# Choosing 16 experts of 16384, tile by tile and from 80 candidate pairs, in a two-block model kernel

## What is computed

```python
q = (xb @ w_q).reshape(PEER_BLOCK, PEER_HEADS, 2, PEER_HALF)
s = jnp.einsum('thjd,hjkd->thjk', q, sub_keys).astype(jnp.float32)
sv, si = lax.top_k(s, PEER_TOPK)
cand = sv[:, :, 0, :, None] + sv[:, :, 1, None, :]
cs, ci = lax.top_k(cand.reshape(PEER_BLOCK, PEER_HEADS, PEER_TOPK * PEER_TOPK), PEER_TOPK)
i1 = jnp.take_along_axis(si[:, :, 0], ci // PEER_TOPK, axis=-1)
i2 = jnp.take_along_axis(si[:, :, 1], ci % PEER_TOPK, axis=-1)
eidx = i1 * PEER_N_KEYS + i2
g = jax.nn.softmax(cs, axis=-1)
act = jax.nn.gelu(jnp.einsum('td,thkd->thk', xb, expert_u[eidx]), approximate=False)
return jnp.einsum('thk,thkd->td', (g * act), expert_v[eidx])
```

## Time and profile before

| | us |
|---|---|
| three runs | 2925.65, 2932.58, 2934.63 |
| median | 2932.58 |
| profiled execution: its time | 2928.44 |
| profiled execution: span from first to last instruction | 2926.6 |
| busy: PE, DVE, POOL, ACT | 2019.9, 1854.2, 1261.4, 638.5 |
| chain that ended last | PE 41%, DVE 23%, DMA 13%, issue 10%, POOL 7%, ACT 5% |
| moved by DMA | 797.62 MB, of it 536.94 by gathers |

### The profile page before, as it was taken

How to read it: one execution, slowest core, us unless ns; L and a number is a source line. 1 busy time by engine, 2 the same in 40 slices (tenths; PEclk the granted TensorE clock), 3 DMA queues, 4 the chain that set the end, 5 groups by cost and what they waited for, 6 DMA issues and landing times.

```text
span 2926.6 us, 26514 instructions
## 1 busy us (share of the span) xinstructions
PE 2019.9 (69%) x9256; PEld 1629.7 (56%) x9256; DVE 1854.2 (63%) x3630; ACT 638.5 (22%) x1713; POOL 1261.4 (43%) x1060
## 2 busy tenths in 40 slices
PE   7999989860887787796550031246348899993898
PEld 6888878750776676785440021234346555443685
DVE  2333310198688899867799978888976566754200
ACT  4555520110443433200210020011012200002210
POOL 0000000006576666566655656767755675641000
PEclk8999989985899888897875566665777999996899
DMA  4332324334799999899897579999987899984176
GB/s 165 110 128 108 115 94 146 109 141 171 259 353 368 347 361 370 330 414 382 316 378 266 183 278 411 358 362 335 387 321 282 322 381 390 406 322 172 63 253 245
DMA packets 178871, 797.62 MB, mean 273 GB/s; under 512 B 20001, under 2 KB 20257, under 8 KB 153137
## 3 DMA queue, kind: packets, MB, share of 16 engines
q0 software_dynamic: 147456, 536.94, 48.7%
q1 hardware_dynamic: 30704, 256.89, 23.1%
q10 hardware_dynamic: 576, 2.10, 0.2%
HBM read 793.75 MB, written 2.10 MB: 272 GB/s over the span
## 4 chain that ended last, share of the span: by engine, by line
PE 41%; DVE 23%; DMA 13%; issue 10%; POOL 7%; ACT 5%; DVEq 0%; ACTq 0%
PE ps L678 41%; DMA ring<-in_pu,eidx 9%; POOL ring L650 7%; DMA ring<-in_pv,eidx 3%; DVE acc L1833 3%; DVE junke L1833 3%; DVE junke L1827 2%; DVE acc L1827 1%; DVE si L1415 1%; DVE tmpx L1485 1%; DVE ci L1415 1%; DVE sv L1413 1%; DVE cv L1413 1%; ACT L1032 1%; ACT L1030 1%
## 5 line engine op out<-in xcount | busy, mean ns | idle before, releaser
L650 POOL DMA_INDIRECT ring<-in_pu,eidx x512 | 654.4, 1278 | 366.0 <-DVE dots L1827 221.3
L650 POOL DMA_INDIRECT ring<-in_pv,eidx x512 | 575.2, 1124 | 367.7 <-DVE acc L1833 121.5
L678 PE MATMUL ps<-uT,wr 128*128 128x256 f32 (+1 forms) x2304 | 533.6, 388 | 2.8 <-ACT ynT L1212 2.8
L678 PEld LDWEIGHTS ps<-uT,wr 128*128 128x128 f32 x2304 | 440.4, 193 | 72.1 <-issue 3.3
L678 PE MATMUL ps<-hT,wr 128*128 128x128 f32 (+2 forms) x1984 | 406.0, 369 | 8.7 <-ACT hT L1071 7.1
L678 PE MATMUL ps<-junk,h 128*128 128x128 f32 x256 | 49.5, 380 | 484.6 <-DVE junk L1436 484.6
L678 PEld LDWEIGHTS ps<-hT,wr 128*128 128x128 f32 x1984 | 304.1, 198 | 109.9 <-issue 8.1
L1827 DVE CUSTOM_DVE_ANT_0 junke<-ring,u 128x1024 f32<-128x1024 f32 x256 | 312.7, 1222 | 62.8 <-DMA ring<-in_pu,eidx 60.1
L1827 DVE CUSTOM_DVE_ANT_0 acc<-ring,u 128x1024 f32<-128x1024 f32 x256 | 313.0, 1222 | 43.2 <-DMA ring<-in_pu,eidx 40.3
L1833 DVE SCALAR_TENSOR_TENSOR acc<-ring,wgt,acc 128x1024 f32<-128x1024 f32 x252 | 324.9, 1289 | 12.1 <-DMA ring<-in_pv,eidx 12.0
L1833 DVE SCALAR_TENSOR_TENSOR junke<-ring,wgt,junke 128x1024 f32<-128x1024 f32 x252 | 325.0, 1290 | 8.3 <-DMA ring<-in_pv,eidx 8.2
(11 more groups left out here) (260 smaller groups left out, 2502.5 us busy)
## 6 DMA issues: line engine op xcount, KB each, us to landing
wr<-in_wg SPq DMA_DIRECT2D x32, 1536.0 KB, 9.0
wr<-in_wgu SPq DMA_DIRECT2D x44, 1024.0 KB, 6.2
wr<-in_wsc SPq DMA_DIRECT2D x16, 1536.0 KB, 8.5
wr<-in_wso SPq DMA_DIRECT2D x16, 1536.0 KB, 8.2
wr<-in_wq SPq DMA_DIRECT2D x16, 1152.0 KB, 5.4
wr<-in_wqku SPq DMA_DIRECT2D x18, 1024.0 KB, 8.2
wr<-in_wdn SPq DMA_DIRECT2D x12, 1536.0 KB, 7.9
wr<-in_wgate SPq DMA_DIRECT2D x16, 1024.0 KB, 5.0
```

What stands on the lines that cost most here:

```text
L650: e.indirect_dma_start(ring[k % NR][:], None, A[which], bass.IndirectOffsetOnAxis(ap=eidx[:, t, j:j + 1], axis=0)).then_inc(gathered[k % N ...
L678: return e.matmul(o, l, r, start=start, stop=stop, skip_group_check=True)
```

## The change

- A `top` unit now belongs to one tile and one head: `top16` on three pieces, that head's two halves (128 values) and the *preceding* head's pairs (80 values). The unit of head 0 has no pairs; a new unit `toplast` does those of head 7 alone. The unit `pairs` is gone.
- The 256 sums become 80 in three pieces: the best of the first half with all 16 of the second (16), the next 7 with the first 8 (56), the last 8 with the best (8). `ci` then is a place among the 80, and `slots` decodes it into the two places with ten small operations; `first` loses its two.
- Only the first tile of a pass is searched while PE makes scores. The second tile's eight `top` units and its `toplast` follow after the first tile's `index`, with the experts that the planner finds between them.

The planner's counts of experts ahead of a unit:

| unit | before | now |
|---|---|---|
| `index` of tile 1 | 13 | 45 |
| start of mixer pass 1 | 16 | 48 |
| end of its scan | 244 | 273 |
| start of choice 1 | 358 | 390 |
| first `top` of choice 1 | 367 | 399 |
| `index` of tile 2 / of tile 3 | 479 / 493 | 472 / 513 |
| start of attention of tiles 0, 1 | 512 | 516 |
| start of attention of tile 2 / of feed-forward 0 to 2 | 769 / 825 | 773 / 829 |
| last unit of that feed-forward | 1005 | 1009 |

The core of the diff:

```diff
         if hj % 2:
-            pl.add("top", q, hj // 2, v=2 * nt * 5 * (0.1 + 128 / 960.0))
-            yield True
-            pl.add("pairs", q, hj // 2, v=nt * (vc(32) + vc(256) + 5 * (0.1 + 256 / 960.0)))
+            pl.add("top", q, hj // 2, t0, v=10 * (0.1 + 128 / 960.0) + 5 * (0.1 + 80 / 960.0) + 0.6)
             yield True
     for t in range(t0, t1):
+        for h in range(0 if t > t0 else 8, 8):
+            pl.add("top", q, h, t, v=10 * (0.1 + 128 / 960.0) + 5 * (0.1 + 80 / 960.0) + 0.6)
+            yield True
+        pl.add("toplast", q, t, v=1.5)
...
+                    q, h, t = (u[1], u[2], u[3]) if kind == "top" else (u[1], 8, u[2])
                     m = CH[q]
+                    i = t - MIXERS[q][0]
+                    then()
+                    parts = []
+                    if h < 8:
+                        w.wait_ge(*act.at("score", q, 2 * h + 1))
+                        parts = [(m["sv"][:, i, 2 * h + j, :], m["si"][:, i, 2 * h + j, :],
+                                  m["s_sb"][:, 2 * h + j, 128 * i:128 * i + 128]) for j in range(2)]
+                    if h:
+                        one, two = m["sv"][:, i, 2 * h - 2, :], m["sv"][:, i, 2 * h - 1, :]
+                        cand = m["cand"][:, h % 2, :]
+                        e.tensor_copy(m["sif"][:, i, 2 * h - 2:2 * h, :], m["si"][:, i, 2 * h - 2:2 * h, :]
                                       ).then_inc(*dve.up())
+                        e.tensor_tensor(cand[:, 0:16], two, one[:, 0:1].to_broadcast([128, 16]), ADD
                                         ).then_inc(*dve.up())
+                        e.tensor_tensor(cand[:, 16:72].rearrange("p (a b) -> p a b", a=7), b3(one[:, 1:8], 8),
+                                        bmid(two[:, 0:8], 7), ADD).then_inc(*dve.up())
+                        e.tensor_tensor(cand[:, 72:80], one[:, 8:16], two[:, 0:1].to_broadcast([128, 8]), ADD
+                                        ).then_inc(*dve.up())
+                        parts.append((m["cv"][:, i, h - 1, :], m["ci"][:, i, h - 1, :], cand))
+                    top16(parts)
...
-                    e.tensor_scalar(m["cu1"][:], m["ci"][:, i], 15, None, ALU.bitwise_and).then_inc(*dve.up())
-                    then()
-                    e.tensor_copy(cx[:], m["cu1"][:]).then_inc(*dve.up())
+                    e.tensor_scalar(m["cu0"][:], m["ci"][:, i], 3, None, ALU.logical_shift_right).then_inc(*dve.up())
+                    e.tensor_scalar(m["cu1"][:], m["ci"][:, i], 7, None, ALU.bitwise_and).then_inc(*dve.up())
+                    then()
+                    e.tensor_copy(unit[:], m["cu0"][:]).then_inc(*dve.up())
+                    e.tensor_copy(place[:], m["cu1"][:]).then_inc(*dve.up())
+                    then()
+                    e.scalar_tensor_tensor(out=last[:], in0=unit[:], scalar=9.0, in1=place[:], op0=ALU.is_equal, op1=MUL
+                                           ).then_inc(*dve.up())
+                    e.tensor_scalar(second[:], unit[:], 1.0, 8.0, ALU.is_equal, MUL).then_inc(*dve.up())
+                    e.tensor_scalar(first[:], unit[:], 1.0, 0.0, SUB, ALU.max).then_inc(*dve.up())
+                    then()
+                    e.tensor_tensor(cx[:], place[:], last[:], SUB).then_inc(*dve.up())
+                    e.tensor_tensor(first[:], first[:], last[:], ADD).then_inc(*dve.up())
+                    then()
+                    e.tensor_tensor(cx[:], cx[:], second[:], ADD).then_inc(*dve.up())
...
-                    e.tensor_scalar(m["cu0"][:], m["ci"][:, i], 4, None, ALU.logical_shift_right).then_inc(*dve.up())
...
-                    e.tensor_copy(cx[:], m["cu0"][:]).then_inc(*dve.up())
```

More of the change, by code:

```diff
@@ L553, in build @@
                 ab("sif", [128, nt, 16, 16])
-                ab("cand", [128, nt, 256])
+                ab("cand", [128, 2, 80])
                 ab("cv", [128, nt, 8, 16])
@@ L561, in build @@
                     ab(f"cx{i}", [128, 8, 16])
+                for i in range(4):
+                    ab(f"cy{i}", [128, 8, 16])
                 ab("rd", [128, 8])
@@ L1595, in vector @@
                     e.tensor_tensor(hv, hv, b[:, 0:256], ADD).then_inc(*dve.up("wo", q, hf, t))
-                elif kind == "top":
-                    _, q, h = u
+                elif kind in ("top", "toplast"):
+                    q, h, t = (u[1], u[2], u[3]) if kind == "top" else (u[1], 8, u[2])
                     m = CH[q]
[L1600 to L1608, removed]
-                    then()
-                    for t in range(nt):
-                        e.tensor_copy(m["sif"][:, t, 2 * h:2 * h + 2, :], m["si"][:, t, 2 * h:2 * h + 2, :]
+                    i = t - MIXERS[q][0]
+                    then()
+                    parts = []
[7 more added lines that the diff above has]
+                        e.tensor_copy(m["sif"][:, i, 2 * h - 2:2 * h, :], m["si"][:, i, 2 * h - 2:2 * h, :]
@@ L1612, in vector @@
                                       ).then_inc(*dve.up())
-                    for t in range(nt):
-                        e.tensor_tensor(m["cand"][:, t, :].rearrange("p (a b) -> p a b", a=16),
-                                        b3(m["sv"][:, t, 2 * h, :], 16), bmid(m["sv"][:, t, 2 * h + 1, :], 16), ADD
+                        e.tensor_tensor(cand[:, 0:16], two, one[:, 0:1].to_broadcast([128, 16]), ADD
                                         ).then_inc(*dve.up())
-                    top16([(m["cv"][:, t, h, :], m["ci"][:, t, h, :], m["cand"][:, t, :]) for t in range(nt)])
+                        e.tensor_tensor(cand[:, 16:72].rearrange("p (a b) -> p a b", a=7), b3(one[:, 1:8], 8),
+                                        bmid(two[:, 0:8], 7), ADD).then_inc(*dve.up())
@@ L1622, in vector @@
                     i = t - MIXERS[q][0]
-                    oh, cx = m["oh1"], m["cx1"]
+                    oh, cx, first = m["oh1"], m["cx1"], m["cx0"]
+                    unit, place, last, second = (m[f"cy{i_}"] for i_ in range(4))
                     then()
-                    e.tensor_scalar(m["cu1"][:], m["ci"][:, i], 15, None, ALU.bitwise_and).then_inc(*dve.up())
+                    e.tensor_scalar(m["cu0"][:], m["ci"][:, i], 3, None, ALU.logical_shift_right).then_inc(*dve.up())
+                    e.tensor_scalar(m["cu1"][:], m["ci"][:, i], 7, None, ALU.bitwise_and).then_inc(*dve.up())
                     then()
-                    e.tensor_copy(cx[:], m["cu1"][:]).then_inc(*dve.up())
+                    e.tensor_copy(unit[:], m["cu0"][:]).then_inc(*dve.up())
[10 more added lines that the diff above has]
+                    e.tensor_tensor(cx[:], cx[:], second[:], ADD).then_inc(*dve.up())
                     then()
```

## The result

The changed kernel takes 2949.82 us, median of 6 runs (2943.86 to 2956.36); the kernel before, run with it, 2929.47. The ratio is 1.0071, 95% interval 1.0055 to 1.0087: slower, by 20.4 us between the medians. The profiled executions are 19.5 us apart, 2947.91 and 2928.44. The forecast was 2946 us, range 2930 to 2963.

The account below looks back on a forecast made before the run. The prediction took DVE's fixed sequence as the bound, except PE in the first choice and transfers in the output products. Its terms summed to +15.3 us, 2943.7 on the profiled execution, forecast as 2946 us, range 2930 to 2963.

Parts of the forecast that it names:

- (a): First choice: tile 0's slot arithmetic starts 19.6 us sooner, longer decoding takes back 1.4; -18.2 us.
- (b): Before the second mixer pass: tile 1's choice now stands in DVE's way, searches 31.9 us and decoding 1.4; +33.3 us.
- (c): Ahead of the second mixer pass: 48 experts, not 16, at 1.15 us each; +36.8 us, to come back later.
- (d): Behind tile 1's slots: the run of experts grows from 12 to 14, the ring holds 8; +2 us (0 to 7).
- (e): Second mixer pass: scan -3.5 for fewer experts, +10.2 for the end of tile 0; output products +4.0; +10.7 us.
- (f): Second choice to tile 1's last expert: fewer experts -37.9, searches -13.3, decoding +2.8, tile 3's numbers -2.8, waits +2; -49.2 us.
- (g): Behind tile 1's end: tile 3's numbers +2.8, the 2.56 us wait for the next norm's squares goes; +0.2 us.
- (h): Four experts more ahead of the attention, +4.6, and 4 fewer behind the feed-forward, -4.9; -0.3 us.
- 1: Rival: transfers also pace the second pass's first part and hide the moved end of tile 0; 2934 us; 0.20 with 4.
- 4: Rival: the gather stream is the only bound from 660 us on, the early gain is spent again; near 2934 us; 0.20 with 1.
- 2: Rival: short operations don't scale, 2961 us, or gathers starve the new stretch, 2956 us; chance 0.15.
- 3: Rival: over 24.1 of 44.8 us of DVE's waits for rows in the attention go; 2916 us with 30 gone; chance 0.08.

Follow-up runs that it names:

- late16: Changed kernel with the planner's costs of tile 1's searches set to nothing, 16 experts ahead of the second mixer pass; 2949.07 us, ratio 1.0051.
- pairs80: Kernel before with 80 candidates and the longer decoding, both tiles together, order of work unchanged; 2915.98 us, ratio 0.994.
- spread: pairs80 with the planner's cost of the second choice's pair search halved for heads 1 and 2, 1.25 times for heads 4 to 7; 2908.11 us, ratio 0.9924.
- tile256: Changed kernel, in its order, with 256 candidates and the old decoding; 2982.09 us, ratio 1.0155.
- heavy14: Kernel before with the planner's weight of a tile 0 expert 1.4 for 1.5, putting the end of tile 0 inside the scan; 2955.77 us, ratio 1.0061.
- light17: Kernel before with the planner's weight of a tile 0 expert 1.7 for 1.5; 2937.65 us, ratio 0.9996.
- keep42: Changed kernel with the planner's weight of a tile 0 expert 1.7 for 1.5, end of tile 0 behind the scan; 2938.69 us, ratio 1.0025.

## Why the forecast held, step by step

Measured against the steps of the sum, from the two profiled executions:

| step | forecast | measured |
|---|---|---|
| (a) tile 0 sooner | -18.2 | -19.1, of it 0.8 from an earlier start of the stage (563.1 for 563.9) |
| (b), (c), (d) between tile 0's numbers and the pass | +72.1 | 118.97 - 46.96 = +72.0 |
| (e) second mixer pass | +10.7 | +7.4 (scan +6.0, output products +1.4) |
| (f) second choice, first search to end of tile 1 | -49.2 | 244.98 - 288.78 = -43.8 |
| (g), (h) behind it | -0.1 | +8.9 to the next norm, -6.0 by the end: +2.9 |
| sum | +15.3 | +19.5 |

(a), and (b) to (d) together, are right to a microsecond; the 3.9 us of a unit stand in the timeline as 3.85, and with them the line that gave the step at 80 values. The idle DVE is the price of the order, as forecast, and late16 against pairs80 shows it by itself: about 27 us in the first choice, 25 of them waits for `s_sb`. What the forecast did not ask is how much of (a) the order brings at all: narrowing alone has 14.4 of the 19.1 us (pairs80). (c) was to come back from later stretches, and does: 28 experts fewer in the second choice give 30.3 us (late16 against the changed kernel), and 4 fewer in the feed-forward behind the attention were to give the rest of 36.8.

(e) had the right cause. The end of tile 0 inside the scan costs 6.4 to 14.7 us in four kernels, 9.5 in the changed one against 10.2 forecast; the output products rose by 1.4 instead of 4.0, because three things nearly cancel there: the end of tile 0 gone (-10.2), three experts more (+3.5) and 8 us more of waits for rows (47.7 for 39.6 over the same stage, 1185:1407). I had counted the first as hidden by the third and priced the experts at the transfers' pace.

(f) is the mis-sized term, and the largest miss of the sum. I put +2 for waits for rows and it was 7.6; pairs80 has 5.9 of the same kind beside a DMA share of 1.00, and spread, which moves up to four experts away from the weights, has 2.8. My mean of 340 GB/s over 114 us hid a stretch that is full, the 40 us at 414 GB/s shown above.

(g) was wrong: the wait for the norm's squares did not vanish (2.56 us at 1752.37, as before), because at a stage's border ACT holds the squares back (`fence` in the kernel) until DVE has done all that stands ahead of the border, tile 3's numbers and the experts among it:

```profile
1738.61 0.20 ACT L1036 ACTIVATE se<-se 128x1 f32<-128x1 f32 x1
1749.91 1.06 ACT L1060 ACTIVATE junk<-h 128x1024 f32<-128x1024 f32 x1 [11.10 <-DVE dots L1847]
```

The step took the squares as free to start once tile 1 was finished (ACT's work before them ended at 1738.81); they start 0.09 us behind DVE's last expert ahead of the border. In the kernel before the end of tile 1 was itself DVE's last work there, and the wait the same 2.56 us. So tile 3's numbers cost their 2.8 us in full. The other 6 us to that norm are four experts and the row that opens tile 2. By the end of the span 6 us have come back, which leaves +2.9 for (g) and (h) together.

The hit is in part luck: (e) came 3.3 us cheaper than forecast and (f) with (g) and (h) 8.4 dearer, and the sum stayed in the range. The same terms without the experts that move (late16) missed by 10 us, and the forecast saving of the narrowing alone (pairs80) by 7. The direction and its main cause are shown; a microsecond of the total is not.

The rivals: 1 and 4 (transfers or the gather stream set the pace and hide the move) fall with the scan's +6.0 us at three experts fewer and a DMA share of 0.89. 2 falls with 3.85 us for a unit, 2.24 for the decoding and 2.09 for the lone pair search; of its other form, starving gathers, 3.4 us appeared before the pass. 3 (waits in the attention go) does not occur: 42.1 us for first-half rows against 44.8.

As a ledger from the ratios: narrowing the search -0.6%, the order +1.1%, and 32 experts ahead of the pass with the end of tile 0 in the scan +0.2%, together the +0.7% measured. The last of these is the difference of two ratios whose intervals overlap (late16 1.0031 to 1.0071, changed 1.0055 to 1.0087), and rests on the stages more than on them. That the three are independent was not tested beyond tile256, where narrowing is worth 0.8% and not 0.6.

## What to carry to other kernels

An early start of one consumer is worth only what the engine that sets the pace does not lose for it: here splitting two tiles brought the first numbers 5 us further forward than the narrower search alone does, and for that left the vector engine idle 4 us in each head, then did the second tile's work with nothing beside it. When work is interleaved by a planner's costs, look at what a changed count pushes across a stage border; here ten microseconds of dependent steps were nearly free in a stretch that transfers fill and cost 6 to 15 in one that the engine fills. And a cheaper operation beside full transfers can lose part of its saving to waits for rows, here about half: place the transfers first, then count the saving.

## What the runs showed of the hardware that I had not expected

The attention of tiles 0 and 1, the same work in every kernel, took between 413.5 and 423.5 us by profile, a spread larger than several of the effects studied here, and partly by chip; only ratios on one chip could settle those. And the granted clock of PE in the scan, as a share of full speed, goes down as its length goes up: 0.84 at 481 us (heavy14), 0.86 at 456 and 462 (before, changed), 0.89 and 0.90 at 425 and 419 (light17, keep42), with the same 1688 products; whether it causes any of the difference was not tried.
